# Expert inputs in a two-layer diffusion step: the 512 latent tokens as one moving operand, the 128 prompt tokens as stationary side once for four chunks of weights

## The reference, cut to what matters

```python
def block(xb):
    q = (xb @ wq).reshape(tb, PEER_HEADS, 2, PEER_DK // 2)
    sc = jnp.einsum('thsd,hskd->thsk', q, subkeys).astype(jnp.float32)
    sv, si = lax.top_k(sc, PEER_TOPK)
    ...
    idx = i1 * N_KEYS + i2
    gsm = jax.nn.softmax(best, axis=-1)
    ue = u_tab[idx]
    act = jax.nn.gelu(jnp.einsum('td,thkd->thk', xb, ue))
    ve = v_tab[idx]
    return jnp.einsum('thk,thkd->td', (gsm * act).astype(ve.dtype), ve)
```

## Time and profile before

| | |
|---|---|
| median of 3 runs | 4794.67 us (4794.41 to 4800.49) |
| the profiled execution | 4797.76 us, span 4796.0 us, mean granted clock 0.969 |
| PE, DVE, POOL, ACT busy | 93%, 69%, 54%, 25% of the span |
| layer 0: early, late and tail, values | about 580 to 983, 994 to 1600, 1602 to 2414 us |
| layer 1: early, late and tail, values | about 2976 to 3379, 3390 to 3998, 3999 to 4776 us |

### The profile page before, as it was taken

The page is one execution under the profiler, slowest core; times in us unless marked ns, Lnnn a source line. Parts: engine busy times, 40 slices in busy tenths (PEclk is TensorE's granted clock), DMA queues, the critical chain, the costliest instruction groups (busy, mean ns, idle before and its releaser), DMA issues.

```text
span 4796.0 us, 76065 instructions
## 1 busy us (share of the span) xinstructions
PE 4458.9 (93%) x27516; PEld 4027.5 (84%) x27516; DVE 3310.5 (69%) x6141; ACT 1176.9 (25%) x1696; POOL 2571.5 (54%) x1462
## 2 busy tenths in 40 slices
PE   7888999999999999999789889999999999999996
PEld 6758999999999877777577689999999998877775
DVE  6872299779998577777734422992799984555555
ACT  2052011123233222222133420111232322222222
POOL 2413455644444688888731134555444446778874
PEclk9879999999999999999898999999999999999998
DMA  5401244557777877778510012444577778777774
GB/s 198 168 1 58 72 121 121 191 125 157 160 159 156 289 273 273 270 277 280 206 70 24 23 58 72 121 121 121 126 156 161 160 156 272 262 262 262 262 259 148
DMA packets 823653, 797.69 MB, mean 166 GB/s; under 512 B 566513, under 2 KB 601041, under 8 KB 822898
## 3 DMA queue, kind: packets, MB, share of 16 engines
q1 hardware_dynamic: 175248, 500.38, 31.2%
q10 hardware_dynamic: 603106, 159.70, 15.5%
q0 software_dynamic: 45056, 134.38, 8.7%
HBM read 640.41 MB, written 153.89 MB: 166 GB/s over the span
## 4 chain that ended last, share of the span: by engine, by line
PE 50%; POOL 18%; ACTq 8%; issue 7%; DVE 6%; DMA 6%; ACT 4%; DVEq 0%; POOLq 0%
PE acc L514 14%; PE acc L516 13%; PE acc L515 13%; POOL w_lo L487 10%; POOL found L463 5%; DMA pick_act<-act_p,where_i 5%; ACTq L1047 4%; ACTq L1080 4%; POOL pick_act L469 3%; PE aux L729 2%; ACT w_hi L1113 1%; ACT gates L1097 1%; PE aux L572 1%; DVE ag L1539 1%; PE aux L679 1%
## 5 line engine op out<-in xcount | busy, mean ns | idle before, releaser
L514 PE MATMUL acc<-a_hi,w_hi 128*128 128x320 f32 x5296 | 1670.1, 315 | 45.5 <-DVE a_lo L1287 32.5
L516 PE MATMUL acc<-a_hi,w_lo 128*128 128x320 f32 x5296 | 1641.0, 310 | 0.2 <-issue 0.2
L515 PE MATMUL acc<-a_lo,w_hi 128*128 128x320 f32 x5296 | 1640.6, 310 | 0.0
L514 PEld LDWEIGHTS acc<-a_hi,w_hi 128*128 128x128 f32 x5296 | 999.6, 189 | 50.9 <-issue 34.6
L515 PEld LDWEIGHTS acc<-a_lo,w_hi 128*128 128x128 f32 x5296 | 999.8, 189 | 1.4 <-issue 0.2
L516 PEld LDWEIGHTS acc<-a_hi,w_lo 128*128 128x128 f32 x5296 | 998.2, 188 | 0.5 <-issue 0.5
L438 POOL TENSOR_TENSOR w_lo<-w_in,w_hi 128x1024 fp32r<-128x1024 f32 (+1 forms) x345 | 902.1, 2615 | 27.6
L454 POOL CAST w_hi<-w_in 128x1024 fp32r<-128x1024 f32 x256 | 309.8, 1210 | 1044.3 <-DMA w_in<-in_u 1044.3
L487 POOL TENSOR_TENSOR w_lo<-w_in,w_hi 128x1024 fp32r<-128x1024 f32 x256 | 655.1, 2561 | 201.7 <-ACT w_hi L1113 198.4
L1525 DVE SCALAR_TENSOR_TENSOR one_b<-iota_b,picks_t 128x384 bf16<-128x384 bf16 x1024 | 629.8, 615 | 0.0
L1523 DVE TENSOR_SCALAR one_a<-iota_b,picks_t 128x128 bf16<-128x128 bf16 x1024 | 579.6, 566 | 56.6 <-PE aux L729 54.6
(11 more groups left out here) (246 smaller groups left out, 5682.7 us busy)
## 6 DMA issues: line engine op xcount, KB each, us to landing
w_in<-in_u SPq DMA_DIRECT2D x256, 512.0 KB, 4.1
w_in<-in_v SPq DMA_DIRECT2D x256, 512.0 KB, 5.9
gate_s<-gates ACTq DMA_DIRECT2D x64, 1024.0 KB, 14.1
ag<-act_s SPq DMA_DIRECT2D x256, 256.0 KB, 4.2
ag<-gate_s SPq DMA_DIRECT2D x256, 256.0 KB, 5.0
act_s<-a_out ACTq DMA_DIRECT2D x184, 256.0 KB, 3.7
act_s<-tmp ACTq DMA_DIRECT2D x72, 256.0 KB, 3.2
w_in<-in_in SPq DMA_DIRECT2D x32, 512.0 KB, 5.8
```

The lines of the kernel that those rows point to most:

```text
L514: pe.matmul(out, wh, hi[:, k, n], start=(k == 0), stop=False)
L515: pe.matmul(out, wh, lo[:, k, n], start=False, stop=False)
L516: return pe.matmul(out, wl, hi[:, k, n], start=False, stop=(k == kt - 1))
```

## The change

- **Latent tokens.** A chunk's stationary slices now meet all 512 latent tokens in one matmul: 24 matmuls of 512 columns a chunk, into `acc[0][:, m % 2]`. The groups of gates stand after 12 and after 24 of them.
- **Prompt tokens.** After every fourth chunk a new step `prompt` makes the prompt's product for four chunks (512 experts) at once: the tokens are the stationary operand, the weights of four slots the moving one, 24 matmuls of 512 columns into `acc[1][:, bank]`. ACT applies the gelu once for the four and stores 128 rows of 2 KB to `act_p`, which now lies token by token.
- **Slots.** Slots are counted from each layer's first "u" chunk, so that four chunks lie side by side. Since the prompt step reads all four, their slots come free together: loads of "u" chunks wait for `made_p` instead of `made`, and so do the first 8 loads of "v".
- **Small moves.** The index arithmetic for the gathers (`where`) stands ahead of the softmax on DVE; `act_p`'s layout changes its formula; the gathers wait for the prompt stores (`p_st`) alone; near the end of the inputs ACT's casts of the first "v" chunks are moved, those of slots 4 and 5 behind the end of the inputs.

```diff
+def slots():
+    slot, before, loads, had = [], [], [], {}
+    start = {l: next(n for n, c in enumerate(CHUNKS) if c[:2] == (l, "u")) for l in range(2)}
+    for n, chunk in enumerate(CHUNKS):
+        w = (n - start[chunk[0]]) % SPLIT
...
@@ last_use
+            if kind == "u":
+                return made_p, NKEY // GROUP * layer + i // GROUP + 1
             return made, past
@@ SP
-                def load_inputs(c, u):
-                    slot = (UC[l] + u) % SPLIT
-                    sp.wait_ge(made, UM[l] - SPLIT + 1 + c)
+                def load_inputs(i, u):
+                    if isinstance(i, int) and i == 0:
+                        sp.wait_ge(*last_use(BEFORE[UC[l] + u]))
+                    else:
+                        sp.wait_ge(made_p, FOURS * l + u // GROUP - 1 + 2 * i)
@@ PE
-                    for h in range(2):
-                        n = slice(h * HALF, (h + 1) * HALF)
-                        for k in range(KD):
-                            mm = linear_step(acc[m0 % 2][:, h, 0:HALF], w, P, k, KD, a_hi, a_lo, n)
+                    spots = [KD * (j + 1) // beside - 1 for j in range(beside)]
+                    for k in range(KD):
+                        mm = linear_step(acc[0][:, m0 % 2, :], w, P, k, KD, a_hi, a_lo, slice(P, T))
...
+                def prompt(g, first_slot, bank):
+                    w, n = slice(first_slot, first_slot + GROUP), slice(0, P)
+                    for k in range(KD):
+                        wh, wl = w_hi[:, w, k * P:(k + 1) * P], w_lo[:, w, k * P:(k + 1) * P]
+                        pe.matmul(acc[1][:, bank, :], a_hi[:, k, n], wh, start=(k == 0), stop=False)
+                        pe.matmul(acc[1][:, bank, :], a_lo[:, k, n], wh, start=False, stop=False)
+                        mm = pe.matmul(acc[1][:, bank, :], a_hi[:, k, n], wl, start=False, stop=(k == KD - 1))
+                    mm.then_inc(made_p, 1)
@@ ACT
-                    act.dma_start(act_p_rows[l][bass.ds(c, 1)].rearrange("o p n -> (o p) n"), out[:, 0:P])\
-                       .then_inc(a_st[slot], 16)
+                def prompt(g, k):
+                    act.wait_ge(made_p, FOURS * l + g + 1)
+                    act.activation(p_out[k][:], acc[1][:, k, :], ACT.Gelu_apprx_tanh).then_inc(taken_p, 1)
+                    act.wait_ge(taken_p, FOURS * l + g + 1)
+                    act.dma_start(act_p_rows[l][:, bass.ds(4 * P * g, 4 * P)], p_out[k][:]).then_inc(p_st[k], 16)
...
-                        act.wait_ge(made, UM[l] + NKEY)
+                        act.wait_ge(made_p, FOURS * (l + 1))
```

More of the change, by code:

```diff
@@ L49 @@
 CHUNKS, PRODUCTS = plan()
+def slots():
[3 more added lines that the diff above has]
+        w = (n - start[chunk[0]]) % SPLIT
+        last, count = had.get(w, (None, 0))
+        slot.append(w)
+        before.append(last)
+        loads.append(count + 1)
+        had[w] = n, count + 1
+    return slot, before, loads
+SLOT, BEFORE, LOADS = slots()
 def chunk_at(layer, kind):
@@ L97, in build @@
         iota_b = sb("iota_b", [P, P], BF)
+        mask_at = end[0]
         mask = sb("mask", [P, 384])
@@ L234, in build @@
         act_in = [sem(f"act_in{i}") for i in range(2)]
+        made_p, taken_p = sem("made_p"), sem("taken_p")
+        p_st = [sem(f"p_stored{i}") for i in range(2)]
         part_ready, added, total_turned = sem("part_ready"), sem("added"), sem("total_turned")
@@ new lines, in early @@
+                def early(i):
+                    for u in range(SPLIT):
+                        expert(UM[l] + u, u, UC[l] + u + 1 + SPLIT * i, (UM[l] + u) // 2 + (SPLIT // 2) * i)
+                        if u % GROUP == GROUP - 1:
+                            prompt(2 * i + u // GROUP, u // GROUP * GROUP, u // GROUP)
+                for m in (UM[l] - 2, UM[l] - 1):
+                    has_taken(pe, m)
+                early(0)
+                with pe.Fori(1, EARLY) as i:
+                    early(i)
@@ L773, in values @@
                                     has_taken(pe, m)
+                            if first and u == 0 and dt == 6:
+                                pe.wait_ge(taken_p, FOURS * (l + 1))
                             mm = value_step(dt, u, first and u == 0, False)
@@ L1060, in early @@
                                    m0 // 2 + 1 + 4 * i, SPLIT * i + u)
+                        if u % GROUP == GROUP - 1:
+                            prompt(2 * i + u // GROUP, u // GROUP)
                 early(0)
@@ L1125, in experts @@
                     m0 = UM[l] + c
-                    if c == NKEY - 1:
-                        high_p(0, 0)
                     activation(c % 4, m0, m0 + 1, late_stores(c), m0 // 2 + 1, c)
-                    if c >= NKEY - 6:
-                        high_v(0, c - NKEY + 6)
+                    if c % GROUP == GROUP - 1 and c < NKEY - 1:
+                        prompt(c // GROUP, c // GROUP % 2)
+                    if c in (NKEY - 3, NKEY - 2):
+                        for u in range(2):
+                            high_v(0, 2 * (c - NKEY + 3) + u)
+                high_p(0, 0)
+                prompt(FOURS - 1, 1)
                 high_p(0, 1)
                 for u in range(2, SPLIT):
-                    if u >= 6:
+                    if u >= 4:
                         high_v(0, u)
@@ L1483, in route @@
                 ins.then_inc(shifted, 1)
+                step(dve.scalar_tensor_tensor(where[:, 0, :], picks[:, 1, 0, :], float(P), picks[:, 0, 0, :],
+                                              ALU.mult, ALU.add))
+                step(dve.tensor_scalar(where[:, 1, :], where[:, 0, :], tok[:, 0:1], None, ALU.add))
+                if l:
+                    step(dve.tensor_scalar(where[:, 0, :], where[:, 0, :], float(NKEY * P), None, ALU.add))
+                dve.tensor_copy(where_i[:], where[:]).then_inc(where_ready, 1)
                 if l == 0:
```

123 lines of the change are left out of this document (65 added, 58 removed).

## The result

The change makes the kernel slower: 5001.12 us (median of 4 runs, 4995.79 to 5010.38) against 4795.49 us for the kernel before on the same chip, a ratio of 1.042 [1.041, 1.044]. The profiled execution took 4995.8 us (span 4994.0), 198 us more than the one of before. The forecast of "slower" holds, and so do the place and the cause that it named; its 4925 is 76 us short, and 5001 lies just outside the range of 4810 to 4995.

What follows compares the result with a forecast made beforehand. PE was taken to bound the early stage, PE and DVE together the late stage, POOL, DVE and gathers the values. 4797.8 - 27 - 3 + 150 + 12 = 4930, against the median 4927, stated as 4925 us; range 4810 to 4995.

Steps and rivals of the forecast that it cites:

- The step that failed: Late stage, four POOL splits back to back: DVE makes two tokens per split, 2.16 us each, in a 17.3 us burst.
- upper bound: Late stage: one token per split chunk in a burst, 4.3 us each; waits 3.8 and 5.9 us, +230 us.
- C: Late stage, third group of gates after a prompt step: ready at 9.6 us, PE waits 0.1 us.
- D: Late stage, fourth group of gates after a prompt step: ready at 18.2 us, wanted at 12.9, PE waits 5.3 us.
- E: Late stage, fifth group of gates after a prompt step: ready at 23.5 us, PE there at 21.6, waits 1.9 us.
- late term: Late stage: PE waits 7.3 us per four-chunk cycle, 9.9 us a chunk against 8.73, +150 us over 128 chunks.
- The clock: Late stage, behind the wait at D: a clock fall costs PE some 1.7 us, hidden by the wait for E; nothing added.
- PE's gain: Early stage: 30 matmuls instead of 48 a chunk, 6.80 us against 7.04, saving 27 us over 114 chunks.
- Start of the values: Start of the values stage: gathers and casts come later, PE waits some 6 us a layer, +12 us (bounds 0 and 24).
- That the grouping costs nothing: Late stage: four slots coming free together cost nothing and the kernel gets faster, 4740 to 4775 us; chance 0.11.
- That ACT takes over: Late stage: stores hold ACT's queue, so PE waits 3.8 us for gate copies; 4805 to 4860 us; chance 0.09.
- The fourth rival: Late stage: POOL shuts DVE out fully, 3.46 us a chunk, or bursts pass one token a chunk; 4980 to 5030 us; chance 0.08.

Runs made afterwards that it cites:

- e9_gap: Changed kernel, with POOL waiting for its own result after each subtraction, leaving a short gap before its next cast: 4970.3 us, ratio 1.036.
- e7: Changed kernel, with POOL's splits paced by PE's products so that no two splits touch, loads still in fours: 4844.4 us, ratio 1.010.
- e8: Changed kernel, with the splits paced as in e7 and the gates spread evenly, two groups of them inside the prompt step: 4777.3 us, ratio 0.995.
- e2: Kernel before, with only the loads of input chunks grouped in fours; matmuls, stores and gates as before: 4980.4 us, ratio 1.037.

## Where the prediction held, and the step that failed

**The step that failed** is the one of the late stage that reads: "Beside a working POOL, DVE makes two tokens in 1.47 + 2.85 = 4.32 us", "the burst lasts 17.3 us, to 21.9, at 2.16 us a token". The burst lasts 14.7 us at one token per 3.63 us. The forecast itself had "one token per split chunk in a burst" as its upper bound, with +230 us; +208.7 came out. I preferred the schedule "since each of its durations is a row". They were, but rows of single splits, after which POOL pauses. What a row could not show was who starts first when POOL has the next instruction ready. Put the measured 3.63 us a token and a burst of 14.5 us into the forecast's own count, with the groups 3.47 us apart, and C comes 3.3 us late, D 4.3 and E on time (an estimate from these rows); ten of the 15 cycles have C 3.6 and D 4.3 us late. So the method was sound, and the rate was wrong. That the upper bound came within 21 us is in part luck: it has 4.3 us for a token, and counted as the schedule counts, this rate gives waits of some 5.0 and 5.6 us, about +259 us and not +230.

The table sets the forecast's schedule beside the mean distances of the groups in the late stage of layer 0, all from PE's starts; the unwaited cycle is 7 x 3.47 + 8.91 us.

| us in a cycle (mean of 15) | unwaited | late at C | at D | at E | cycle |
|---|---|---|---|---|---|
| forecast | 32.4 | 0.1 | 5.3 | 1.9 | 39.7 |
| e9_gap | 33.2 | 1.3 | 4.4 | 2.0 | 40.9 |
| after | 33.2 | 3.4 | 4.6 | 0.7 | 41.9 |

e9 is the forecast's schedule made real: 7.7 us of lateness where it said 7.3, at the same three groups. The change has 8.7, moved from E to C. Why so little more, with three tokens fewer in the burst? The burst is over 2 to 3 us earlier, and DVE then makes a token in 0.70 us: it has caught up by E, but C and D needed theirs earlier. In time, the change's late stages less those of e9 are 14.8 + 13.6 = 28 us, of the 59 by which the late term (+150, measured +208.7) was too small.

**The second part of the miss** is PE's own time. The forecast priced a group of gates at 0.65 us, from its start to the next large matmul. But the matmul behind that one comes late too. In the changed kernel, behind group C:

```profile
1278.87 0.48 PE L545 MATMUL acc<-a_hi,w_hi 128*128 128x512 f32 x1
1279.18 0.39 PE L546 MATMUL acc<-a_lo,w_hi 128*128 128x512 f32 x1
1279.41 0.39 PE L547 MATMUL acc<-a_hi,w_lo 128*128 128x512 f32 x1
```

The first distance is 0.31 us, the next 0.23: a group costs 0.65 + 0.08, and a cycle of eight 0.8 us more than my 32.4, 26 us over 32 cycles. This is also why e9 came out above its expectation, which had used the same 32.4: its two late stages are together 22 us longer than 32 x 39.7. In these 22 us are the 26 of the gates and 13 for waits of 7.7 us instead of 7.3, less 17, since the cycle at each end of a stage is not a whole one or hardly waits. The last 8 us of the 59 lie in how the forecast counted: 128 chunks at 8.73 us, 5 us more than the two stages of before in the table, and 1.17 for (39.7 / 4 - 8.73) (3 us). So the 59 are 28 + 22 + 8, within rounding.

The same price of a group corrects the reading of before. There the groups lie 4.26 us apart unwaited, so that PE alone needs 8.52 us a chunk, not 8.34, and it waited only some 0.2 us a chunk, not 0.39. Nor was it DVE that it waited for, as the prediction has it: in the late stages behind their first groups the waits for `one_b` are 0.3 us, those for ACT's copies 12.0, and 8.7 us in four cases have no releaser. DVE was nearly as slow as PE, but its lead hid this. The 32.4 of the forecast's cycle had the same fault. The section on the change, too, has a slip: between two groups of gates PE now streams fewer columns than before, 12 x 512 = 6144 against 24 x 320 = 7680, not more, which is why the groups lie 3.47 us apart and no longer 4.26.

**The clock.** The forecast saw the fall after D and added nothing, since the wait for E would hold that time anyway. Windows with C's wait in them, with D's, and behind D:

```profile
1274.20:1278.20 4.00, 0.56 (x3) 0.14 (x1) 4.00 (x4) 0.55 (x1) 3.89 (x3) 1.00 0.56 92
1278.00:1286.00 8.00, 3.65 (x24) 2.81 (x24) 8.00 (x10) 0.60 (x1) 5.91 (x3) 1.00 0.92 145
1286.00:1296.00 10.00, 9.99 (x63) 8.07 (x64) 8.74 (x26) 2.61 (x3) 0.00 (x0) 0.83 0.47 89
```

The clock stays at the higher level through C's 3.45 us and D's 4.14 us. Behind the wait ahead of D the large matmuls start 0.43 us apart for a few us, the lower level, then 0.23 again. In e9 the 2.0 us at E are filled by such slow matmuls with no idle time left, as the forecast has it; whether DVE alone would have been as late can't be read from that. In the changed kernel DVE is less behind at E, and the mean 0.7 us there, slow matmuls without a wait, are the clock's: 0.7 x 32, some 23 us. It is part of the lateness above, not added to it, and no experiment isolates it.

**Point by point.** PE's gain: forecast -27 us early, measured -30.0, from the start distances of the earlier trace rows. The rows decide against the figure worked out from the Trainium skill (TensorE: Matmul & The Clock Gate, Back-to-back issue gap), which would leave 0.045 us a chunk, 5 us over 114 chunks. Tails: -3, measured -0.4. Of these two, 2.7 us only changed places: a prompt step can't be cut in quarters, and of a layer's 32 steps 14 fall in the early stage and 2 in the tail, where the forecast has 14.25 and 1.75. Turn of the picks: counted as nothing, measured +8.3 us. The six DVE instructions that split the picks take 0.43 to 0.69 us where nothing holds them; now a burst of four splits lies on top of them:

```profile
972.67 2.74 DVE L1581 TENSOR_TENSOR picks_t<-picks_t,part_b 128x512 f32<-128x512 f32 x1
...
976.62 2.45 DVE L1580 CAST part_b<-picks_t 128x512 bf16<-128x512 f32 x1
```

The turn takes 17.2 us; with the splits apart (e7, e8) it is down to 9.9. It is the same cause in a second place, and I had looked for it in one only. Start of the values: +12 forecast, +6.7 measured over the whole stage. The chain is there as written, in layer 0 with the inputs' last matmul, the first gather and `parts`:

```profile
1696.43 0.39 PE L746 MATMUL acc<-w_lo,a_hi 128*128 128x512 f32 x1
...
1715.51 0.96 POOL L500 DMA_INDIRECT pick_act<-act_p,where_i  x1
...
1721.68 0.16 DVE L1633 TENSOR_TENSOR part_now<-pick_act,picks 128x4 f32<-128x4 f32 x1 [10.41 <-DMA pick_act<-act_p,where_i]
```

The inputs end at 1696.8, this gather starts 18.7 us later and `parts` 24.9 us later, against the 6 and 15 that the earlier trace rows give and the 17 to 18 and 27 of the forecast. What it had wrong is PE's wait, some 6 us in each layer: PE stands 2.9 us ahead of its matmul at 1723.29 in layer 0, and in layer 1 not at all in the 30 us behind the first matmul of the values. The rest of the +6.7 has no cause that the traces single out.

Against the profiled execution the forecast was 4930, and 4995.8 came out, 66 us more. They are, each rounded, 59 in the late stage, 8 in the turn, 5 outside the stages, 3 less gained in the tails, 3 more gained early, and 5 less lost at the values.

**The rivals.** That the grouping costs nothing is out by e2. That ACT takes over did not show: the waits of PE for ACT's copies are 2.9 us in 6 cases in layer 0's late stage, all at a weight load, and in e8, where DVE's waits are nearly gone, they are 14.1 us in all and the time isn't the 4805 to 4860 of that rival but 4777. e8 moved the gates too, though, so ACT's case with the gates where the change puts them and DVE quick was not tested alone. The fourth rival, "harder", gave the right time (4980 to 5030) by the second of its two mechanisms, one token a chunk; its first, a stall of 3.46 us a chunk, is not what the rows show: there `one_a` takes 2.37 us and `one_b` 1.42, and a split costs DVE 2.93 us in all. That the +214 us worked out from this 3.46 lies only 5 us from the measured +208.7 is luck, since it has two tokens pass for each split.

## What to carry to other kernels

Work that holds another engine costs by where it lies as well as by its sum: four splits in one burst cost 5001 - 4844 = 157 us against the same four apart, with the same bytes and results, and the same instructions but for one wait on POOL. When an edit frees several buffers at once, look at what the freed buffers start, pace that by the consumer's progress instead of by the arrival of its data, and give the consumer's other inputs no longer pause than the producer's lead bridges. When a schedule is built by hand from single events, test it on the case where the disturbing engine has its next instruction ready.

## What the runs showed of the hardware

- **Who starts first decides, and a pause of 0.2 us changes it.** Back to back, POOL's cast starts 0.03 us ahead of the DVE instruction that follows (1273.11 and 1273.14; 90 of 90 places), and DVE makes a token per 3.63 us; with 0.19 us of idle time on POOL `one_b` is first in 90 of 90, and DVE makes two per 4.30 us. The Trainium skill (SBUF — State Buffer, Who interferes with whom) says that issue order decides who blocks on the shared port pair, and the traces agree. They add that here POOL's instruction started first each time when it was ready.
- **Long waits among dense matmuls brought the lower clock, nearly always.** In the changed kernel's late stages PE has 31 waits of 3.4 to 7.1 us, and with 30 of them the granted clock falls during the wait or within 1 us behind it; the exception is C's 3.45 us above. In e9 it is 30 of 30 (3.5 to 4.9 us). With the nine waits of 1.0 to 2.3 us in the late stages of before it never falls. The time at the lower level is 298 us in the trace of before and 518 us in that of the changed kernel.
- **The pace of float32 pairs is 226.7 ns at 512 columns with either side standing**; the new step's rows (L744 at 1260.17 and at 1264.25, 18 matmuls apart) show it again:

```profile
1260.17 0.39 PE L744 MATMUL acc<-w_hi,a_hi 128*128 128x512 f32 x1
...
1264.25 0.39 PE L744 MATMUL acc<-w_hi,a_hi 128*128 128x512 f32 x1
```
